# A second pair of seven-product blocks in place of two plain windows, in a hybrid encoder layer

## The reference, cut to what matters

```python
h = _rms(x, norm1_g)
q, k, v, c = jnp.split(h @ w_in, ...)          # 8 heads of 64, 2 key/value heads
attn = _window_attention(_rms(q), _rms(k), v, sink)   # keys within +-128, ALiBi, learned sink
u = a * jax.nn.sigmoid(gate)                   # a, gate = split(c, 2)
u = jax.nn.silu(_layernorm(_dwconv(u, conv_dw_w, conv_dw_b)))   # 31 taps along tokens
x = x + jnp.concatenate([attn, u], axis=-1) @ w_out
h2 = _rms(x, norm2_g)
g = jax.nn.silu(_dwconv(h2 @ ffn_w_gate, ffn_dw_w, ffn_dw_b))   # 3 taps along tokens
x = x + (g * (h2 @ ffn_w_up)) @ ffn_w_down
```

## Time and profile before

| | us |
|---|---|
| median of 3 runs (2664.36 to 2668.46) | 2665.61 |
| span of the profiled execution | 2660.9 |
| TensorE busy | 2631.4 (99%) |
| DVE busy | 1820.6 (68%) |
| ScalarE busy | 1258.5 (47%) |

### The profile page before, as it was taken

The page is one execution under the profiler, slowest core; times in us unless marked ns, Lnnn a source line. Parts: engine busy times, 40 slices in busy tenths (PEclk is TensorE's granted clock), DMA queues, the critical chain, the costliest instruction groups (busy, mean ns, idle before and its releaser), DMA issues.

```text
span 2660.9 us, 35240 instructions
## 1 busy us (share of the span) xinstructions
PE 2631.4 (99%) x13191; PEld 2337.7 (88%) x13191; DVE 1820.6 (68%) x3020; ACT 1258.5 (47%) x2031; POOL 192.8 (7%) x332
## 2 busy tenths in 40 slices
PE   8999999999999999999999999999999999999998
PEld 6777777788889988889998889998899999999998
DVE  4775658787686876676876677876257576765764
ACT  6345464566454447345446345446144333533432
POOL 0110021100110000010000010000000000000001
PEclk9999999999999999999999999999999999999999
DMA  9967679633843444843443853433745521222211
GB/s 332 349 227 249 249 280 361 231 128 125 298 165 117 156 132 135 290 167 115 157 136 123 291 169 120 157 129 132 284 157 174 177 64 60 68 65 63 68 52 66
DMA packets 138761, 453.73 MB, mean 171 GB/s; under 512 B 24449, under 2 KB 37121, under 8 KB 121953
## 3 DMA queue, kind: packets, MB, share of 16 engines
q1 hardware_dynamic: 111616, 349.17, 39.0%
q0 software_dynamic: 26976, 102.32, 10.5%
HBM read 362.63 MB, written 88.79 MB: 170 GB/s over the span
## 4 chain that ended last, share of the span: by engine, by line
PE 93%; DVE 3%; issue 1%; DMA 1%; ACT 1%; SPq 0%; POOL 0%; DVEq 0%; ACTq 0%; POOLq 0%
PE bank L2131 31%; PE bank L2147 16%; PE bank L2277 12%; PE bank L2083 12%; PE bank L2117 8%; PE bank L2293 7%; PE bank L2231 2%; PE bank L2209 2%; PE bank L2220 2%; DMA wraw<-w_in_t 1%; DVE weights L1561 0%; PE bank L2176 0%; DMA weight_scratch<-weights 0%; ACT weights L1147 0%; ACT part_hi L1404 0%
## 5 line engine op out<-in xcount | busy, mean ns | idle before, releaser
L2131 PE MATMUL bank<-hw_hi,weights 128*128 128x440 f32 (+1 forms) x2816 | 812.2, 365 | 0.0
L2131 PEld LDWEIGHTS bank<-hw_hi,weights 128*128 128x128 f32 x2816 | 530.0, 188 | 47.9 <-issue 12.9
L2131 PE MATMUL bank<-hw_lo,weights 128*128 128x440 f32 (+1 forms) x1408 | 510.8, 363 | 0.0
L2147 PE MATMUL bank<-mid,weights 128*128 128x438 f32 x2112 | 431.9, 364 | 0.0
L1561 DVE TENSOR_TENSOR weights<-wraw,weights 128x1024 fp32r<-128x1024 f32 x286 | 348.8, 1220 | 117.0 <-ACT weights L1147 116.8
L2147 PEld LDWEIGHTS bank<-mid,weights 128*128 128x128 f32 x2112 | 396.0, 189 | 33.3 <-issue 7.6
L1147 ACT ACTIVATE weights<-wraw 128x1024 fp32r<-128x1024 f32 x286 | 301.5, 1054 | 256.9 <-DMA wraw<-w_down_t 171.2
L1668 DVE SCALAR_TENSOR_TENSOR cc<-win,par,cc 128x512 f32<-128x512 f32 x600 | 414.5, 744 | 0.0
L2083 PE MATMUL bank<-h_hi,weights 128*128 128x512 f32 x1104 | 358.6, 398 | 2.9 <-DVE weights L1561 2.9
L2131 PEld LDWEIGHTS bank<-hw_lo,weights 128*128 128x128 f32 x1408 | 264.4, 188 | 16.6 <-issue 1.0
L2083 PEld LDWEIGHTS bank<-h_hi,weights 128*128 128x128 f32 x1104 | 207.9, 188 | 56.0 <-issue 8.3
(11 more groups left out here) (213 smaller groups left out, 3688.0 us busy)
## 6 DMA issues: line engine op xcount, KB each, us to landing
weights<-weight_scratch SPq DMA_DIRECT2D x88, 1024.0 KB, 5.9
wraw<-w_ffn_t SPq DMA_DIRECT2D x176, 512.0 KB, 3.5
wraw<-w_down_t SPq DMA_DIRECT2D x88, 512.0 KB, 3.5
weight_scratch<-weights POOLq DMA_DIRECT2D x22, 1024.0 KB, 8.3
part_raw<-w_ffn_t SPq DMA_DIRECT2D x88, 256.0 KB, 2.6
part_raw<-w_pass_t SPq DMA_DIRECT2D x44, 256.0 KB, 2.6
cat_hi<-cat_scratch SPq DMA_DIRECT2D x10, 1024.0 KB, 6.6
cat_lo<-cat_scratch SPq DMA_DIRECT2D x10, 1024.0 KB, 9.0
```

What stands on the lines that cost most here:

```text
L2131: mm = nc.tensor.matmul(out, l[:, k, :], r[:, k, 1:TC + 1] if s else r[:, k, :], start=(k == 0 and j == 0), stop=(k == KT - 1 and j == 2))
L2147: mm = nc.tensor.matmul(out, l[:, q, :], mid[:, k, part, :], start=(k == 0 and j == 0), stop=(k == FH - 1 and j == 2))
```

## The change

`PLAIN` goes from 4 to 2 and `PAIRS` from 1 to 2: two plain windows of 450 columns and two blocks of two windows of 416. There are 242 slots and 396 steps of products. The order of halves is now written out, the last O comes between the last G and D slots, attention, convolution and LayerNorm get earlier and denser places, and memory is laid out anew: the residual of chunk 4 has a place of its own, the ring of high weight parts has 4 buffers. Maxima operations are done once for two score tiles. The gate's first tap is done by ScalarE from PSUM; its bias goes into the swish. Keys and values are loaded apart. For the second block, windows are loaded as the last group of the first one frees its parts, and summed and split from 7 steps before its first product on.

```diff
-PLAIN, PAIRS = 4, 1
-TP = 406
+PLAIN, PAIRS = 2, 2
+TP = 416
...
-for _w in range(PLAIN):
-    PHASES.append(("F", _w, 0))
-    if _w + 1 < CHUNKS:
-        PHASES.append(("O", _w + 1))
-    PHASES.append(("F", _w, 1))
+PHASES += [("G", 0, 0), ("D", 0, 0), ("O", 1), ("G", 0, 1), ("D", 0, 1), ("O", 2)]
+PHASES += [("G", 1, 0), ("D", 1, 0), ("O", 3), ("G", 1, 1), ("O", 4), ("D", 1, 1)]
...
-ATTN_AT = {0: (16, 10), 1: (59, 10), 2: (103, 20), 3: (178, 20), 4: (252, 20)}
-CONV_AT = {0: (12, 47), 1: (58, 96), 2: (108, 165), 3: (181, 240), 4: (256, 312)}
+ATTN_AT = {0: (16, 10), 1: (57, 10), 2: (99, 10), 3: (139, 10), 4: (180, 9)}
+CONV_AT = {0: (12, 47), 1: (58, 84), 2: (95, 128), 3: (139, 171), 4: (182, 209)}
...
-LN_STEPS = {c: tuple(LN_SUM[c] + i for i in ((1, 1, 2, 2, 3, 3, 4, 4, 5) if c < 2 else (1, 2, 3, 4, 5, 6, 7, 8, 9)))
+LN_STEPS = {c: tuple(LN_SUM[c] + i for i in (1, 1, 2, 2, 3, 3, 4, 4, 5))
             for c in CONV_AT}
...
-        POOL_SIDE[_b - 2].append(("load_kv", _c))
+        if _c > 0:
+            POOL_SIDE[_b - 2].append(("load_k", _c))
+        POOL_SIDE[_b + 1].append(("load_v", _c))
...
-        ACT_SIDE[_b + _t + 2].append(("exp", _N, _t))
+        ACT_SIDE[_b + (3, 4, 5, 5)[_t]].append(("exp", _N, _t))
...
+WINDOW_STEPS = [(-7, "sum T1"), (-6, "low B11"), (-6, "sum T2"), (-5, "low T1"), (-5, "sum T3"), (-4, "sum T4"),
+                (-3, "low T2"), (-3, "low B21"), (-2, "low B22"), (-1, "low T3"), (0, "low T4")]
-HI_RING, DOWN_RING = 5, 4
+HI_RING, DOWN_RING = 4, 4
...
-        for _i, _t in enumerate(("T1", "T2", "T3", "T4")):
-            DVE_AT[_n - 6 + _i].append(("window_sum", _q, _t))
         for _i, _b in enumerate(B_ORDER):
-            ACT_AT[_n - 6 + _i].append(("window_high", _q, _b))
-            DVE_AT[_n - 6 + _i].append(("window_low", _q, _b))
+            ACT_AT[_n - 7 + _i].append(("window_high", _q, _b))
+        for _i, _w in WINDOW_STEPS:
+            DVE_AT[_n + _i].append(("window_sum" if _w[:3] == "sum" else "window_low", _q, _w[4:]))
...
+        x2_last, = run(R_SIDE - H, ("x2_last", [P, KT, TB], F32))
+        x2 = [x2_first] * (CHUNKS - 1) + [x2_last]
...
-                nc.scalar.activation(gb[J % 2][:], bank[out_bank(OUTPUT["G", w, h, i, 0])][:, 0:TH], ACT.Copy) \
-                  .then_inc(s_gb, 1)
+                f = FH * h + i
+                src = bank[out_bank(OUTPUT["G", w, h, i, 0])]
+                if J >= 2:
+                    act.wait_ge(s_mlo, J - 1)
+                nc.scalar.activation(cv[J % 2][:], src[:, 0:TC], ACT.Copy, scale=col("ffn_w", FFN_TAPS * f)).then_inc(s_c1, 1)
+                nc.scalar.activation(gb[J % 2][:], src[:, 0:TH], ACT.Copy).then_inc(s_gb, 1)
...
-                nc.scalar.activation(cv[J % 2][:], cv[J % 2][:], ACT.Silu).then_inc(s_sl, 1)
+                nc.scalar.activation(cv[J % 2][:], cv[J % 2][:], ACT.Silu, bias=col("ffn_b", FH * h + i)).then_inc(s_sl, 1)
...
+                if t % 2 == 0:
+                    return
+                two = slice(KV_HEADS * (t - 1), KV_HEADS * (t + 1))
+                done = GROUP // 2 * N + t // 2
                 dve.wait_ge(s_sb, HEADS * N + KV_HEADS * (t + 1))
-                nc.vector.tensor_tensor(m4[i][:, at], mx[i][:, at], sinks[:, at], ALU.max).then_inc(s_m4, 1)
+                nc.vector.tensor_tensor(m4[i][:, two], mx[i][:, two], sinks[:, two], ALU.max).then_inc(s_m4, 1)
...
-                nc.vector.tensor_scalar(t[:], gb[J % 2][:, 0:TC], col("ffn_w", FFN_TAPS * f), col("ffn_b", f),
-                                        ALU.mult, ALU.add).then_inc(s_c1, 1)
                 dve.wait_ge(s_c1, J + 1)
```

More of the change, by code:

```diff
@@ L95 @@
         SLOT += [("O", _p[1], o) for o in range(KT)]
+    elif _p[0] == "G":
+        SLOT += [("G", _p[1], _p[2], i // 2, i % 2) for i in range(GU_TILES)]
     else:
-        SLOT += [("G", _p[1], _p[2], i // 2, i % 2) for i in range(GU_TILES)]
         SLOT += [("D", _p[1], _p[2], i) for i in range(D_TILES)]
@@ L260, in conv_room @@
     kind = SLOT[n][0]
-    tile = {"A": 0.4, "O": 1.8, "G": 2.1, "D": 0.6}[kind]
+    tile = {"A": 0.4, "O": 1.8, "G": 1.6, "D": 0.6}[kind]
     if n + AHEAD < SLOTS and SPLIT[n + AHEAD]:
@@ L611, in encoder_layer @@
-        m_at = R_MID
-        y_at = [R_MID + M_BYTES + Y_BYTES * i for i in range(2)]
-        b_at.append(R_HW - B_BYTES)
-        assert R_D + 4 * B_BYTES + 3 * E_BYTES <= R_MID and R_HW + 13 * W_BYTES <= R_SIDE
-        assert v_at[2] + V_BYTES <= R_D and R_SM <= b_at[13] and y_at[1] + Y_BYTES <= b_at[13]
-        b_raw, b_lo, b_hi = {}, {}, {}
-        for i, b in enumerate(B_ORDER):
-            lo_at, hi_at = b_at[i], b_at[7 + i]
-            b_raw[b], = run(lo_at, (f"{b}_raw", [P, KH, TQ], F32))
-            b_lo[b], = run(lo_at, (f"{b}_lo", [P, KH, TQ], F32R))
-            b_hi[b], = run(hi_at, (f"{b}_hi", [P, KH, TQ], F32R))
@@ L622, in encoder_layer @@
-        b_raw["B12"] = b_raw["T3"]
-        w_place = {("A", 0, a): i for i, a in enumerate(("A11", "S1", "S2", "A12", "S4", "S3"))}
-        w_place["A22", 0] = 6
-        w_hi_at = w_at[7:7 + HI_RING]
-        w_rest = w_at[7 + HI_RING:]
-        w_places = [("A", 1, a) for a in ("A11", "S1", "S2", "A12", "S4", "S3")] + [("A22", 1), ("A22", 2)] + \
-            [("D", i) for i in range(DOWN_RING)]
-        w_offset = {k: w_at[i] for k, i in w_place.items()}
-        w_offset.update({k: w_rest[i] for i, k in enumerate(w_places)})
+        LATE = R_SIDE - H
@@ new lines, in encoder_layer @@
+        ring_end = B_BYTES + 11 * W_BYTES
+        late_end, side_end = LATE + 3 * B_BYTES, R_ATTN + 6 * B_BYTES
+        lo_at = dict(zip(B_ORDER, [R_D + B_BYTES * i for i in range(4)] + [R_ATTN + B_BYTES * i for i in range(3)]))
+        hi_at = dict(B11=R_ATTN + 3 * B_BYTES, T1=R_ATTN + 4 * B_BYTES, T2=R_ATTN + 5 * B_BYTES, B21=LATE, B22=0,
+                     T3=LATE + B_BYTES, T4=LATE + 2 * B_BYTES)
+        e_at = [R_D + 4 * B_BYTES + E_BYTES * i for i in range(3)]
+        m_at = e_at[2] + E_BYTES
@@ new lines, in encoder_layer @@
+        y_at = [m_at + M_BYTES + Y_BYTES * i for i in range(2)]
+        w_hi_at = [R_SM + W_BYTES * i for i in range(HI_RING)]
+        w_first = [R_SM + W_BYTES * (HI_RING + i) for i in range(5)] + [side_end, side_end + W_BYTES]
+        w_rest = [B_BYTES + W_BYTES * i for i in range(11)] + [late_end]
+        v_at = [ring_end, late_end + W_BYTES, side_end + 2 * W_BYTES, y_at[1] + Y_BYTES]
+        assert ring_end + V_BYTES <= R_D and w_first[4] + W_BYTES <= LATE and R_SM + HI_RING * W_BYTES >= R_HW
@@ new lines, in encoder_layer @@
+        assert v_at[1] + V_BYTES <= R_ATTN and v_at[3] + V_BYTES <= R_SM
+        b_raw, b_lo, b_hi = {}, {}, {}
+        for b in B_ORDER:
+            b_raw[b], = run(lo_at[b], (f"{b}_raw", [P, KH, TQ], F32))
+            b_lo[b], = run(lo_at[b], (f"{b}_lo", [P, KH, TQ], F32R))
+            b_hi[b], = run(hi_at[b], (f"{b}_hi", [P, KH, TQ], F32R))
+        b_raw["B12"] = b_raw["T3"]
+        w_offset = dict(zip([("A", 0, a) for a in ("A11", "S1", "A12", "S3")] + [("A22", 0), ("A", 0, "S2"), ("A", 0, "S4")], w_first))
@@ L632, in encoder_layer @@
+        w_offset.update(zip([("A", 1, a) for a in ("A11", "S1", "S2", "A12", "S4", "S3")] + [("A22", 1), ("A22", 2)] +
+                            [("D", i) for i in range(DOWN_RING)], w_rest))
         p_raw, p_lo = {}, {}
@@ L992, in _ @@
                         load_residual(c)
-                if n in PAIR_LOADS:
-                    load_pair_window(0, PAIR_LOADS[n])
+                for b in PAIR_LOADS.get(n, ()):
+                    load_pair_window(0, b)
                 if n == LAST + GU_TILES:
@@ L1830, in part_sum @@
                     dve.wait_ge(s_used, SLOTS)
+                elif gi == 0 and a == "S1":
+                    dve.wait_ge(s_ast, 32 * BLOCKS * CHUNKS)
                 two = {"S1": ("A21", "A22"), "S2": ("S1", "A11"), "S3": ("A21", "A11"), "S4": ("A12", "S2")}[a]
```

149 lines of the change are left out of this document (77 added, 72 removed), and 7 rows, old and new, of the table PAIR_DVE.

## The result

The changed kernel takes 2695.03 us (median of 4 runs, 2693.63 to 2699.03) beside 2664.99 us of the kernel before on the same chip: ratio 1.011, 95% interval 1.0098 to 1.0122. It is 1.1% slower. The forecast was 2626 us (2616 to 2636), faster; the measured time is 69 us above it, outside the range, and on the other side of the kernel before. First the page's lines, which answer to the earlier trace rows.

The account below looks back on a forecast made before the run. TensorE was taken as the bound, busy 2631.4 of 2660.9 us. Work -48.3, pinches +6 and seam +3 sum to -39.3, so 2665.6 - 39.3 = 2626 us, range 2616 to 2636.

Parts of the forecast that it names:

- TensorE work, -48.3 us: Matmuls: two plain windows go (634.4 us), a second block comes (545.9), widening adds 24.3 and 15.9; net -48.3 us.
- weight-load floor: Rival: weight loads set the pace of products, so widening is free; 2586 us, chance 0.02.
- The seam, +3: Between the blocks, the second's windows are subtracted and split during the first's last down tiles; overflow taken as +3 us.
- The ring, 0: High weight parts shrink from 5 buffers to 4; a split waits one product (2.2 us) longer, claimed cost 0.
- 0 to 0.5, within the 6: Attention block: first tile's exp waits a slot for the second's scores; 0 to 0.5 us, inside the +6 for pinches.
- The pinches, 4 x 1.5 us: ScalarE where LayerNorm of chunks 1 to 4 meets attention in gate tiles: 1.5 us each, +6 in all.
- my upper bound of 5.5: Most one LayerNorm-attention meeting could cost: 3.7 us added work, a 1.28 table load, 0.5 of a shifted exp.
- The slower one: Rival: VectorE's waits in the middle stage don't compress, holding TensorE 76 us; 2696 us, chance 0.05.
- Its turning point: Needed VectorE idle per middle-stage slot at which that rival turns the change's sign: 1.55 us.
- The dear pinches: Rival: four LayerNorm-attention meetings at 5.5 us instead of 1.5, and a seam of 5; 2644 us, chance 0.14.
- no table switch costs more than its load: ScalarE table switches cost only their 1.28 us load; the rival doubling that gave 2667 us, chance 0.01.

Follow-up runs that it names:

- experiment 13: Kernel of experiment 5 with side work placed by a count, chunk 0's convolution in its old slots, no value product beside a norm's sum: 2642.2 us, ratio 0.991.
- Experiment 6: Experiment 3's kernel with exponentials and maxima as before the change, transposes and values as changed: 2680.8 us, ratio 1.0055.
- experiment 5: Changed kernel with first-pass additions ahead of splits and the earlier attention block (chunk 4 keeps tight transposes), convolution table moved along: 2672.6 us, ratio 1.0019.
- after: The changed kernel itself, against the kernel before: 2695.03 us, ratio 1.011.
- experiment 9: Experiment 5's kernel with the plain gate's swish replaced by a copy, leaving out swish and bias: 2657.8 us, ratio 0.9967.
- experiment 3: Changed kernel with the down tiles' additions put ahead of the splits on VectorE in each block's first pass: 2679.3 us, ratio 1.006.
- experiment 15: Changed kernel with experiment 13's placing of attention blocks, convolution and LayerNorms alone: 2671.3 us, ratio 1.002.
- experiment 16: Experiment 13's kernel with first-pass additions behind the splits again: 2655.4 us, ratio 0.9963.
- experiment 2: Kernel before with the changed attention block (bunched exponentials, paired maxima, three transposes a slot, earlier values): 2686.3 us, ratio 1.0082.

## Why the prediction was wrong

- **TensorE work, -48.3 us: right.** The paces were 205.5 and 190.5 to 190.9 ns; in experiment 13 the blocks are 562.5 and 558.9 against 558.1 each. No sign of a weight-load floor.
- **The seam, +3: 0.** TensorE did not wait there.
- **The ring, 0: it cost 8 us on the kernel before, and 13 to 16 can be had back here.** The step that failed is "with three products of lead, and ScalarE stands in step with the products anyhow for its copies: 0". It counted the lead among products. In the first pass's down tiles a tile fills all four of its output banks, and the addition that frees them stood in VectorE's order behind the split that the smaller ring delays.
- **The attention block was priced at "0 to 0.5, within the 6", for the exponentials alone; the three transposes a slot and the earlier values had no term.** This is the step that failed most plainly: 22 us on the kernel before, 7 to 16 here. Experiment 6 puts 8 to 10 us on the transposes and values; the exponentials, to which I gave the 0.5, showed no cost there.
- **The pinches, 4 x 1.5 us: mis-sized.** The count by slots of experiment 5, which has the additions ahead and, but for chunk 4, the attention block of before, is 65 against 10. The place was partly right (LayerNorm beside attention in gate tiles, slots 90 and 177), but they are dearer than my upper bound of 5.5 (6.6 at slots 90 and 91, 6.6 at 177 and 178). These two are 13 of the 65. I did not look at where the changed table puts the convolution: 10 operations in a slot before the first gate tiles, 12 in one of O(3) (15 in experiment 5), where VectorE is busy 97% of 30 us, nor at shared banks (6.1 at slot 119 of experiment 5, 2.6 at slot 86 of after). The placing, which moves all of this, is worth 24 to 30 us. The price of 1.5 was taken from the loss of one row at 79% load and used at 94%.
- **A wait is paid more than once.** Nothing in my sum had a slower clock behind a wait; after has 37 us at 1.2 GHz among its slots.
- **The rivals.** The slower one gave 2696 us and the measured time is 2695; that is luck, as its mechanism did not act: it held that the middle's average is too dense for VectorE's waits. In experiment 13 VectorE is busy 771.19 of 979.93 us, 79%, and TensorE is idle only 17 us there. Its turning point was also misworked: 1.55 us of idle a slot leaves out its own 26 us for the gate chains, with them it is 1.39. The dear pinches are the nearest of the rivals, but their four places hold only part of the loss, and they had no term for the ring, the transposes or the convolution's table. That no table switch costs more than its load was right: the next operation starts 0.01 us behind it. The Trainium skill ("ScalarE: Activation LUTs", "Rules for kernel authors") has work grouped by table; experiment 9 agrees with the direction, 15 us. The traces set a limit to it: experiment 3 has 46 loads at its exponentials and gate swishes, the kernel of 5 has 54 and is faster; with the new placing, experiment 15 has 42 and experiment 16, with 53, is 16 us faster. Which engine is late in which slot mattered more than their number.

What is open: how much of experiment 13's 30 us is the even convolution, how much the shared bank and how much LayerNorm's longer steps, as they were moved together (the count bounds the shared bank: slots 119 and 129, the only ones of experiment 5 with it, lose some 9 us); whether five buffers would have saved the changed kernel's 16 us, which was not run; and how much of the 65 us is clock. Of its 16 us above the forecast, the count by slots (32.2 against 10.2 + 6) holds all.

## What to carry to other kernels

An average load says nothing of side work that is dealt out to slots: count each engine's work slot by slot against TensorE's slot, and look for shared banks, before a denser layout is judged. A share of 95% over 30 us was free here, and a third transpose that reads what ScalarE writes in the same slot cost 2 to 4 us each time, and so did value products that shared a bank with a norm's sum. When a ring gets smaller, follow every instruction that stands behind the newly delayed one in its engine's order, in the phase where banks are scarcest. Price every moved line of a diff, also those that only change a slot number.

## What was not expected of the hardware

After a wait in the middle of dense work TensorE's granted clock stood at 0.5 for 3.4 or 6.8 us (0.50 over 1164.90 to 1171.70, behind 16.1 us with 4.0 idle; 0.51 over 1594.90 to 1598.30). The kernel before has such a stretch, apart from its start and the time behind its last matmul, only at 2612 us. In the faster kernel of experiment 13 one is left among the slots. Not every wait is followed by one: slot 135 of experiment 13 loses 3.6 us, slots 172 and 247 of experiment 2 lose 3.6 and 3.4, and the granted clock stays at 1.00.
